# A three-layer network in one launch: the first stage cut into quarters of the features, layer 1's mask on the vector engine, three orders at the tail

## The chip, the cores and the metric

One core of a Trainium2 chip (trn2) runs the whole program in one launch. The metric is the device time of the execution in microseconds (us); lower is better. The kernel before took 763.97 us, the median of 3 runs (763.23 to 764.12). Five engines work side by side, each through its own list of instructions in order: TensorE (PE, with its weight loads PEld), VectorE (DVE), ScalarE (ACT), GpSimd (POOL) and SyncE (SP), which here issues the weight transfers.

## The reference, cut to what matters

The input x is 256 tokens by 1024 features. Each layer normalises x, scales and shifts it by rows made from a conditioning vector c, and projects it. Only the start of layer 0 and the score mask of layer 1 matter here; a third part (mixer and feed-forward) follows.

```python
def rms_norm(x, g):
    return x * rsqrt(mean(x * x, -1) + EPS) * g
...
cond  = silu(c) @ w_ada[layer] + b_ada[layer]     # 3 x 1024: shift, scale, gate
h     = rms_norm(x, norm_g) * (1 + scale) + shift
proj  = h @ w_in          # layer 0: keys and values first (kc, ks, vc, vs | ka, kw, va, vw, gates), then qa ...
...
s = where(mask, q @ k.T * HEAD_DIM ** -0.5, -inf)  # layer 1: one block of 256 keys, causal
p = softmax(s); o = p @ v
x = x + gate * (o * silu(z)) @ w_out
```

## The kernel before

**Numbers.** Every float32 operand of a large product is held as a high part and a low part (`WH`, `WL` for weights, `HH`, `HL` for activations), and one product is three matmuls (`product`, lines 456 to 458). ACT makes the high part with a copy, DVE the low part with a subtraction.

**Pieces.** Weights come in pieces of 128 x 2048 numbers (1 MiB), in the order of `piece_table`. SP issues them in that order; a piece goes either into a ring of three slots (`RAW`) or into a tile that is idle then (`areas`). Before it issues a piece, SP waits until the former user of that place is read (`readers`, `low_done`, `follows`), and everything behind it waits too. `highs(n)` on ACT and `lows(n)` on DVE make the high and low parts of all split pieces up to the n-th (in this order: kcks half 0, kakw half 0, kcks half 1, kakw half 1, then qa half 0 as the fifth and qa half 1 as the sixth).

**First stage (0 to 49 us).** The eight 1 MiB pieces of `ada0_0` to `ada0_3` hold the columns of shift (0, 1) and scale (2, 3), each piece 512 columns by half of the rows of c. `conditioning_half` multiplies a piece by silu(c) in four row groups of TensorE at once; DVE adds the bias (`row_in`), TensorE turns the row into columns (`columns_of`), DVE makes `MOD` and `ADA` (`modulation`). The normalised x (`XH`) is transposed (`norm_turn`), and ACT applies scale and shift while it reads the banks (`first_evict`), then copies the high part into `HH`; DVE makes `HL` (`low_pair`, `low_norm`). Features 0 to 511 come first: pieces 0.0, 0.1, 2.0, 2.1, then `kcks` half 0 against features 0 to 511, and so on for 512 to 1023. `hold_clock` issues transposes that nobody reads.

**After it.** `pair_turn(0)` transposes the rotated kcks heads of token tile 0 and needs DVE's `rotate("kcks", 0)`, which needs ACT's `values_out(0)`. Behind it on TensorE stand `by_tokens("qa", 0)`, `pair_turn(1)` and `key_turns()`. ACT's list there is `values_out(0)`, `highs(5)`, `values_out(1)`, `values_out2(0)`, `highs(6)`; DVE's list is `rotate("kcks", 0)`, `lows(5)`, `rotate("kcks", 1)`, `lows(6)`, `rotate("kakw", 0)`, `rotate("kakw", 1)`.

**Layer 1's attention.** Heads go in eight pairs. `scores(p)` makes 8 matmuls for a pair and then adds the mask with one matmul for each head (line 646); `peaks` on DVE reads the banks; between two pairs TensorE does a projection of some 5 us or more.

**Tail.** `low_stick(3)` on DVE frees what the last of `branch("ato", 0)`'s four blocks on TensorE waits for. Further on, `hidden_tokens(0, 0)` needs the bank that `add_merged(1, 0)` frees, and `hidden_tokens(1, 0)` needs the low part of both halves of `fi1`.

Of the kernel before, what the change touches and what calls it, by code (L numbers as in the profile page):

```python
# [17 lines left out]
ALU = mybir.AluOpType  # L18
# [3 lines left out]
P = 128  # L22
S = 256
NT = S // P
# [20 lines left out]
def piece_table():  # L45
# [19 lines left out]
    t = ada(0, 0, 2) + [first[0][0]] + ada(0, 1) + [first[0][1]] + ada(0, 3) + list(first[1]) + qa[:1]  # L65
    w1v = two("w1v", 8, 256, "raw")
    t += two("w1k", 8, 256, "raw") + qa[1:] + w1v[:1] + qb + w1v[1:] + za[:1]
# [100 lines left out]
def two_blocks_kernel(nc, weights, x_in, consts_in, late_in, cols_in, bada_in, finalg_in, w2_in, sinks_in, gains_in, out):  # L168
# [12 lines left out]
    with ExitStack() as ctx:  # L181
# [110 lines left out]
        placed_in = [sem(f"placed_in{i}") for i in range(19)]  # L292
# [31 lines left out]
        def col(name):  # L324
# [6 lines left out]
        areas = [("ada0_2", 1, [flat(QT[:, :, :])]), ("ada0_1", 1, [flat(V[:, :, :])]), ("ada0_3", 0, [flat(ZS[:, :, :])]),  # L331
                 ("ada0_3", 1, [flat(PROBS[:, :, :])[:, 0:PIECE]]), ("w1k", 0, [flat(PROBS[:, :, :])[:, 0:PIECE]]),
# [118 lines left out]

        @block.tensor
        def _(pe):
# [29 lines left out]
            def half_tokens(name, half, t, width=512, kind="proj", use=None, heads=None, between=None):  # L483
                use = use or f"{name}.{t}"
                bank = tiles[ps.uses[use][0]] if half else ps.open(pe, kind, use)
                in_two = name == "kcks"
                if in_two:
                    pe.wait_ge(first_low, half + 1)
                    if t == 0:
                        pe.wait_ge(pair_low, half + 1)  # L490
                else:
                    wait_parts(pe, name, half)
                for k, w in enumerate(row_blocks(name, half, width)):
                    if between and k == KB // 4:
                        between()
                    if in_two and k == KB // 4:
                        wait_parts(pe, name, half)
                        if t == 0:
                            pe.wait_ge(ht_low, 2 * half + 1)
# [53 lines left out]
            def norm_turn(n, t):  # L553
                for half in range(2):
                    turn(f"n{n}.{t}.{half}", [XH[:, t, (4 * half + j) * P:(4 * half + j + 1) * P] for j in range(4)],
                         [(x_hat, 2 * n + t + 1)], "score" if n == 0 and t else "turn")
# [8 lines left out]
            def conditioning_half(layer, c, half, kind="proj"):  # L565
# [13 lines left out]
                else:  # L579
                    mark_read(mm, name, half)  # L580

# [35 lines left out]
            def pair_turn(t):  # L617
                pe.wait_ge(v_copied, t + 1)
                turn(f"up.{t}", [KR[:, t, 0, :], KR[:, t, 1, :], VCD[:, t, 0, :, :].rearrange("p a d -> p (a d)"),
                                 VCD[:, t, 1, :, :].rearrange("p a d -> p (a d)")], [(roped, t + 1)], ("turn", "out")[t])  # L620
# [9 lines left out]
            def scores(p):  # L630
                pair = (2 * p, 2 * p + 1)
                banks = [ps.open(pe, "score", f"s.{u}") for u in pair]
                for t in range(NT):
                    for u, bank in zip(pair, banks):
# [4 lines left out]
                        pe.matmul(out_, lhsT=half_of(q, QT, q // 2, t * P, (t + 1) * P),  # L639
                                  rhs=half_of(q, KT, kb, 0, (t + 1) * P), start=(t == 0), stop=False)  # L640
# [145 lines left out]
            def hold_clock(n):  # L786

                for _ in range(n):
                    pe.transpose(tiles[1][:, 0:P], ident, ident)

            pe.wait_ge(ident_in, 16)
            hold_clock(6)
            pe.wait_ge(cact_ready, 1)
            conditioning_half(0, 0, 0, "out")
            for t in range(NT):
                norm_turn(0, t)
            conditioning_half(0, 0, 1)
            conditioning_half(0, 2, 0)
            conditioning_half(0, 2, 1)
            hold_clock(5)  # L800
            pe.wait_ge(sel_set, 1)
            first_columns = ps.open(pe, "out", "ada0.0")
            ps.fill(columns_of(first_columns, 0, 0), "ada0.0")
            hold_clock(18)
            half_tokens("kcks", 0, 0, 512, between=lambda: conditioning_half(0, 1, 0, "out"))
            pe.wait_ge(ht_low, 2)
            half_tokens("kcks", 0, 1, 512)
            conditioning_half(0, 1, 1)
            conditioning_half(0, 3, 0)
# [1667 lines left out]
```

## Time and profile before

| what | value |
|---|---|
| median of 3 runs | 763.97 us |
| the profiled execution | 764.18 us |
| its span, first to last instruction | 762.4 us |
| PE busy | 745.4 us (98%) |
| DVE busy | 497.9 us (65%) |
| ACT busy | 380.3 us (50%) |
| transfers | 146.50 MB, mean 192 GB/s |

"Busy" is the time in which the engine had an instruction in flight, so the 98% says where the work is, not that TensorE runs at its peak. The span leaves out 1.8 us around the first and last instruction. Times below are in us from the start of the span. In a timeline a row is: start, length, engine, source line, operation, destination and sources, count, and in brackets how long the engine had been idle and what released it.

### The profile page before, as it was taken

The page shows a single profiled execution, that of the slowest core. Times are in us where ns is not written, and L with a number is a line of the kernel's source. Part 1 is how long each engine was busy: PE and PEld are TensorE (multiplying, and loading weights), DVE is VectorE, ACT ScalarE, POOL GpSimd, SP SyncE. Part 2 cuts the span into 40 slices and gives each one's busy share as a digit, 9 for nine tenths or more (in the row PEclk, how much of TensorE's full clock was granted, in tenths as well). Part 3 has the DMA queues.
Part 4 walks back from the last instruction along what each step waited for, and adds up shares of the span by engine and source line. Part 5 has one row for each costly group of instructions (what it writes and reads, how often), then busy time and mean ns, then how long its engine had stood idle before and what let it go on. Part 6 is the DMA issues. An engine that isn't in the chain of part 4 may idle for free.

```text
span 762.4 us, 12229 instructions
## 1 busy us (share of the span) xinstructions
PE 745.4 (98%) x5039; PEld 641.5 (84%) x5039; DVE 497.9 (65%) x685; ACT 380.3 (50%) x577; POOL 25.6 (3%) x43
## 2 busy tenths in 40 slices
PE   5999999999999999999999999999999999999998
PEld 3687876478888878788999999999878999999886
DVE  1486769638847757884889999647863735546431
ACT  2564476545354756545543444697453544344330
POOL 3000001001000000013000000000000000000000
PEclk9999999999999999999999999999999999999999
DMA  9995348914366373353745554514453654454511
GB/s 367 422 380 184 153 172 326 400 70 144 123 237 242 111 262 126 111 204 117 273 172 185 197 191 166 192 58 138 152 183 135 229 214 183 152 219 173 213 56 55
DMA packets 21959, 146.50 MB, mean 192 GB/s; under 512 B 2589, under 2 KB 2717, under 8 KB 5393
## 3 DMA queue, kind: packets, MB, share of 16 engines
q1 hardware_dynamic: 20880, 142.62, 50.4%
q0 software_dynamic: 752, 2.06, 0.9%
q10 hardware_dynamic: 272, 1.05, 0.3%
q8 instruction: 40, 0.66, 0.3%
q14 instruction: 15, 0.11, 0.0%
HBM read 144.68 MB, written 1.05 MB: 191 GB/s over the span
## 4 chain that ended last, share of the span: by engine, by line
PE 78%; DVE 2%; issue 2%; ACT 0%; POOL 0%; POOLq 0%; DVEq 0%; ACTq 0%
PE banks L456 23%; PE banks L458 22%; PE banks L457 22%; PE banks L550 3%; PE banks L639 1%; PE banks L574 1%; DVE WL L1686 1%; PE banks L678 1%; PE banks L646 1%; PE banks L923 0%; PE banks L908 0%; PE banks L682 0%; DVE KT L1718 0%; PE banks L927 0%; PE banks L925 0%
## 5 line engine op out<-in xcount | busy, mean ns | idle before, releaser
L1686 DVE TENSOR_TENSOR WL<-RAW,WH 128x2048 fp32r<-128x2048 f32 (+1 forms) x103 | 233.6, 2278 | 60.2 <-ACT WH L1170 59.9
L1170 ACT ACTIVATE WH<-RAW 128x2048 fp32r<-128x2048 f32 (+1 forms) x103 | 195.7, 1906 | 72.6 <-PE banks L458 65.6
L456 PE MATMUL banks<-HH,WH 128*128 128x256 f32 x768 | 217.9, 284 | 0.0
L457 PE MATMUL banks<-HL,WH 128*128 128x256 f32 x768 | 217.3, 283 | 0.0
L458 PE MATMUL banks<-HH,WL 128*128 128x256 f32 x768 | 217.3, 283 | 0.0
L457 PEld LDWEIGHTS banks<-HL,WH 128*128 128x128 f32 x768 | 147.3, 192 | 0.1
L456 PEld LDWEIGHTS banks<-HH,WH 128*128 128x128 f32 x768 | 147.3, 192 | 0.1
L458 PEld LDWEIGHTS banks<-HH,WL 128*128 128x128 f32 x768 | 147.3, 192 | 0.0
L456 PE MATMUL banks<-WH,HH 128*128 128x512 f32 (+1 forms) x320 | 127.7, 399 | 1.9 <-DVE WL L1686 0.8
L458 PE MATMUL banks<-WH,HL 128*128 128x512 f32 (+1 forms) x320 | 124.6, 389 | 0.0
L457 PE MATMUL banks<-WL,HH 128*128 128x512 f32 (+1 forms) x320 | 124.5, 389 | 0.0
L456 PEld LDWEIGHTS banks<-WH,HH 128*128 128x128 f32 x320 | 60.4, 189 | 18.4 <-issue 3.3
L458 PEld LDWEIGHTS banks<-WH,HL 128*128 128x128 f32 x320 | 60.3, 189 | 12.6
L457 PEld LDWEIGHTS banks<-WL,HH 128*128 128x128 f32 x320 | 60.5, 189 | 11.1
L2156 DVE SCALAR_TENSOR_TENSOR QT<-HB,COL,QT 128x256 f32<-128x256 f32 x120 | 49.0, 477 | 0.0
L456 PE MATMUL banks<-WH,AH 128*128 128x512 f32 x88 | 34.8, 396 | 0.0
L457 PE MATMUL banks<-WL,AH 128*128 128x512 f32 x88 | 34.8, 396 | 0.0
L458 PE MATMUL banks<-WH,AL 128*128 128x512 f32 x88 | 34.8, 395 | 0.0
L1285 ACT ACTIVATE PROBS<-banks,NM 128x128 f32<-128x128 f32 x40 | 14.5, 364 | 33.1 <-DVE NM L1849 33.1
L1555 ACT ACTIVATE BIG<-banks,GBH 128x256 f32<-128x256 f32 x24 | 10.1, 470 | 34.0 <-PE banks L458 34.0
L1848 DVE TENSOR_REDUCE NM<-banks 128x2 f32<-128x256 f32 x20 | 8.5, 423 | 28.0 <-PE banks L646 28.0
L1141 POOL TENSOR_TENSOR RS<-MS,HALFNEG 128x1 f32<-128x1 f32 (+2 forms) x14 | 12.9, 922 | 409.8 <-DVE MS L1712 145.5
(295 smaller groups left out, 910.6 us busy)
## 6 DMA issues: line engine op xcount, KB each, us to landing
RAW<-in_weights_dram SPq DMA_DIRECT2D x114, 1024.0 KB, 4.8
BIG<-in_weights_dram SPq DMA_DIRECT2D x6, 1024.0 KB, 6.2
ROTS<-in_weights_dram SPq DMA_DIRECT2D x4, 1024.0 KB, 7.2
PROBS<-in_weights_dram SPq DMA_DIRECT2D x2, 1024.0 KB, 11.6
RAW<-in_weights_dram SPq DMA_DIRECT2D x2, 816.0 KB, 10.3
GATE<-in_weights_dram SPq DMA_DIRECT2D x3, 512.0 KB, 9.7
X<-in_x_dram ACTq DMA_DIRECT2D x1, 1024.0 KB, 6.0
QT<-in_weights_dram SPq DMA_DIRECT2D x1, 1024.0 KB, 13.7
```

The lines of the kernel that those rows point to most:

```text
L456: pe.matmul(out_, lhsT=w[0], rhs=x[0], start=start, stop=False, **more)
L457: pe.matmul(out_, lhsT=w[0], rhs=x[1], start=False, stop=False, **more)
L458: return pe.matmul(out_, lhsT=w[1], rhs=x[0], start=False, stop=stop, **more)
L550: mm = pe.transpose(bank[:, j * P:(j + 1) * P], src, ident)
L574: mm = pe.matmul(bank[32 * k:32 * k + 32, :], lhsT=CACT[:, kk, 1 - row:33 - row], rhs=raw_block(name, half, k), start=first, stop=last)
L1141: pool.tensor_tensor(RS[:, n, 0:w], MS[:, n, 0:w], HALFNEG[:, 0:w], ALU.pow).then_inc(rstds, 1)
L1170: do(act.activation(WH[:, home[n], 0:kb * width], RAW[:, slot[n] % RAW_RING, 0:kb * width], ACT.Copy), high_done)
L1285: do(act.activation(PR[:, u % 4, 0:P], bank[:, 0:P], ACT.Exp, scale=-1.0, bias=NM[:, u, 0:1], accum_out=DEN[:, u, 0:1]))
L1555: ins = act.activation(GT[:, f, :], bank[:, b * S:(b + 1) * S], ACT.Tanh, scale=0.5, bias=GBH[:, f:f + 1])
L1686: do(dve.tensor_tensor(WL[:, home[n], w], RAW[:, slot[n] % RAW_RING, w], WH[:, home[n], w], ALU.subtract), low_done)
L1848: do(dve.tensor_reduce(NM[:, pair, 0], both_scores[:, :, 0:P], AX.X, ALU.min))
L2156: ins = dve.scalar_tensor_tensor(CV[:, b, :], src, wk, CV[:, b, :], ALU.mult, ALU.add)
```

## The change

1. The conditioning pieces are cut the other way: `("ada0_c", half, KB, 256, "columns")`, 256 columns by all rows of c. Two pieces (one of shift, one of scale) now give a quarter q of the features (two blocks of 128). The order of the pieces, their places and the releases change with it.
2. The stage's products go quarter by quarter: two blocks for token tile 0, two blocks for tile 1, for kcks and kakw. The transposed half 1 of x is copied from its bank to `QR` (`first_raw`) and scaled from there.
3. On DVE `lows(5)` stands ahead of `rotate("kcks", 0)`; ACT's list is unchanged there. `qa` half 1 is loaded ahead of `w1k`.
4. Layer 1's causal mask is added by DVE in the banks, one instruction for a pair; the two matmuls of a pair go.
5. Tail: `low_stick(3)` ahead of `lows(branch_first + 7)`; `norm_turn(3, 1)` inside `hidden_tokens(1, 0)`; two splits of fi0 and fi1 earlier on ACT and DVE.

```diff
+    quarter = lambda c, half: [(f"ada0_{c}", half, KB, 256, "columns")]
+    t = quarter(0, 0) + quarter(2, 0) + [first[0][0]] + quarter(0, 1) + quarter(2, 1) + [first[0][1]]
+    t += quarter(1, 0) + quarter(3, 0) + [first[1][0]] + quarter(1, 1) + quarter(3, 1) + [first[1][1]] + qa
...
+            def conditioning_quarter(c, half):
+                row, name, use = c // 2, f"ada0_{c}", f"quarter.{2 * (c % 2) + half}"
...
+                for k in range(KB):
+                    g = 32 * (k % 4)
+                    mm = pe.matmul(bank[g:g + 32, 0:256], lhsT=CACT[:, k, 1 - row:33 - row], rhs=raw_block(name, half, k),
+                                   start=row == 0 and k < 4, stop=row == 1 and k >= 4)
...
+            def quarter_columns(q):
+                bank = ps.open(pe, "out", f"ada0.{q}")
+                ps.wait_drained(pe, f"quarter.{q}")
+                for j in (2 * q, 2 * q + 1):
+                    mm = pe.matmul(bank[:, 0:2 * KB].rearrange("p (u b) -> p u b", u=2)[:, :, j],
+                                   lhsT=ACC[:, j * P:(j + 1) * P], rhs=SEL[:, :], start=True, stop=True)
...
+            def quarter_tokens(name, q, t, width, kind):
...
+                pe.wait_ge(*((low_done, first_low)[q % 2 == 0], split[index[(name, half)]] + 1))
+                pe.wait_ge((pair_low, ht_low)[q % 2], 2 * half + t + 1)
+                for k in (2 * q, 2 * q + 1):
+                    mm = product(bank[:, 0:width], [h[:, k, t * P:(t + 1) * P] for h in (HH, HL)],
+                                 row_blocks(name, half, width)[k % 4], k == 0, k == KB - 1)
...
 # TensorE's order
+            conditioning_quarter(0, 0)
+            first_turn(0, 0)
+            first_turn(1, 0)
+            conditioning_quarter(2, 0)
+            first_turn(0, 1)
+            pe.wait_ge(sel_set, 1)
+            quarter_columns(0)
+            first_turn(1, 1)
+            hold_clock(10)
+            kcks(0, 0)
+            conditioning_quarter(0, 1)
+            kcks(0, 1)
+            conditioning_quarter(2, 1)
+            for t in range(NT):
+                ps.wait_drained(pe, f"n0.{t}.1")
+            hold_clock(4, 4)
+            quarter_columns(1)
+            hold_clock(9, 4)
+            kakw(0, 0)
+            kakw(0, 1)
+            conditioning_quarter(1, 0)
+            kcks(1, 0)
+            conditioning_quarter(3, 0)
+            kcks(1, 1)
+            quarter_columns(2)
+            kakw(1, 0)
+            kakw(1, 1)
+            kcks(2, 0)
+            conditioning_quarter(1, 1)
+            conditioning_quarter(3, 1)
+            kcks(2, 1)
+            quarter_columns(3)
+            kakw(2, 0)
+            kakw(2, 1)
+            kcks(3, 0)
+            kcks(3, 1)
+            kakw(3, 0)
+            kakw(3, 1)
             pair_turn(0)
...
 # ACT's order
             first_highs(0, 0)
             first_evict(0, 0)
+            first_evict(0, 1)
             first_highs(0, 1)
+            for t in range(NT):
+                first_raw(t)
+            first_highs(1, 0)
+            first_evict(1, 0)
+            first_evict(1, 1)
+            first_highs(1, 1)
+            first_evict(2, 0)
             first_highs(2, 0)
+            first_evict(2, 1)
             first_highs(2, 1)
+            first_highs(3, 0)
+            first_evict(3, 0)
+            first_evict(3, 1)
+            first_highs(3, 1)
...
 # DVE's order
+            quarter_modulation(0)
             first_lows(0, 0)
+            low_quarter(0, 0)
+            low_quarter(0, 1)
             first_lows(0, 1)
+            quarter_modulation(1)
+            first_lows(1, 0)
+            low_quarter(1, 0)
+            low_quarter(1, 1)
+            first_lows(1, 1)
+            quarter_modulation(2)
+            low_quarter(2, 0)
             first_lows(2, 0)
+            low_quarter(2, 1)
             first_lows(2, 1)
+            quarter_modulation(3)
+            first_lows(3, 0)
+            low_quarter(3, 0)
+            low_quarter(3, 1)
+            first_lows(3, 1)
+            lows(5)
             dve.wait_ge(params_in, 16)
             rotate("kcks", 0)
-            lows(5)
             rotate("kcks", 1)
...
 # layer 1's mask, in peaks on DVE
+                if by_vector(p):
+                    diagonal = both_scores[:, :, 0:TRI].rearrange("p u (b c) -> p u b c", b=3)[:, :, 0:3:2, :]
+                    mask = const("maskw")[:, 0:P].unsqueeze(1).unsqueeze(1).to_broadcast([P, 2, 2, P])
+                    do(dve.tensor_tensor(diagonal, diagonal, mask, ALU.add))
+                    do.after()
...
 # tail, TensorE, then DVE
             hidden_tokens(0, 0)
-            norm_turn(3, 1)
-            hidden_tokens(1, 0)
+            hidden_tokens(1, 0, lambda: norm_turn(3, 1))
...
             conf(3)
+            low_stick(3)
             lows(branch_first + 7)
-            low_stick(3)
...
-            lows(first_split("fi0") + 1)
+            lows(first_split("fi0") + 2)
             low_banks(3, 0)
-            lows(first_split("fi0") + 2)
             add_merged(1, 0)
+            lows(first_split("fi1") + 1)
             add_merged(1, 1)
-            lows(first_split("fi1") + 1)
+            lows(first_split("fi1") + 2)
             stat_merged(1)
             gained_hat("n3", 1, FFNR)
-            lows(first_split("fi1") + 2)
             low_banks(3, 1)
```

## Rows read from the trace of the kernel before

**Rows 1.** What TensorE waited for, 520 to 582 us: longest, times, total.
```profile
PE banks L456 <- DVE AH L2206: 0.9, 1, 0.9
```
**Rows 2.** Busy time by stretch, with counts, granted clock, DMA share, GB/s.
```profile
core 0: us, PE busy (x) PEld busy (x) DVE busy (x) ACT busy (x) POOL busy (x), PEclk, DMA share, GB/s
11.00:13.00 2.00, 2.00 (x13) 1.87 (x10) 0.61 (x7) 0.00 (x0) 0.00 (x0) 1.00 1.04 434
...
21.85:49.08 27.23, 25.89 (x137) 19.22 (x137) 15.55 (x21) 18.16 (x34) 2.14 (x4) 1.00 1.01 416
49.08:56.45 7.37, 7.37 (x44) 6.31 (x42) 6.87 (x16) 2.11 (x8) 0.00 (x0) 1.00 1.00 357
```
**Rows 3.** Timeline of TensorE, 31 to 63 us.
```profile
31.94 1.06 PE L574 MATMUL banks<-PROBS,CACT 128*32 128x512 f32 x8 [0.93 <-DMA PROBS<-in_weights_dram]
...
43.92 0.39 PE L456 MATMUL banks<-WH,HH 128*128 128x512 f32 x1
...
44.60 0.34 PE L456 MATMUL banks<-WH,HH 128*128 128x408 f32 x1
...
49.08 0.38 PE L550 MATMUL banks<-CST,BIG 128*128 128x128 f32 x2
...
55.44 1.26 PE L550 MATMUL banks<-CST,BIG 128*128 128x128 f32 x10
...
62.54 1.07 PE L736 MATMUL banks<-PROBS,ZS 128*32 128x256 f32 x16
```
**Rows 4.** Timeline of TensorE, 9 to 22 us.
```profile
9.27 1.93 PE L574 MATMUL banks<-RAW,CACT 128*32 128x512 f32 x8 [0.74 <-DMA RAW<-in_weights_dram]
11.13 3.68 PE L550 MATMUL banks<-CST,KT 128*128 128x128 f32 x16
...
18.50 1.02 PE L589 MATMUL banks<-SEL,BIG 128*128 128x2 f32 x8 [0.21 <-DVE BIG L1731]
19.38 2.16 PE L789 MATMUL banks<-CST 128*128 128x128 f32 x18
21.85 0.47 PE L456 MATMUL banks<-WH,HH 128*128 128x512 f32 x1 [0.30 <-DVE HL L1973]
```
**Rows 5.** Timeline of DVE and ACT, 17 to 22 us.
```profile
17.66 0.69 DVE L1731 TENSOR_TENSOR BIG<-BIG,banks 128x512 f32<-128x512 f32 x1 [6.05 <-PE banks L574]
...
18.98 1.06 ACT L1222 ACTIVATE WH<-RAW 128x1024 fp32r<-128x1024 f32 x1 [9.87 <-DMA RAW<-in_weights_dram]
...
19.96 0.81 ACT L1201 ACTIVATE ROTS<-banks,ADA,MOD 128x128 f32<-128x128 f32 x2
20.14 1.23 DVE L1963 TENSOR_TENSOR WL<-RAW,WH 128x1024 fp32r<-128x1024 f32 x1 [0.22 <-ACT WH L1222]
20.80 0.42 ACT L1209 ACTIVATE HH<-ROTS 128x256 fp32r<-128x256 f32 x1
...
21.29 0.42 DVE L1973 TENSOR_TENSOR HL<-ROTS,HH 128x256 fp32r<-128x256 f32 x1
```
**Rows 6.** Timeline of ACT, then of DVE, 42 to 46 us.
```profile
42.92 0.36 ACT L1347 ACTIVATE ZS<-banks 128x256 f32<-128x256 f32 x1
...
43.34 1.91 ACT L1170 ACTIVATE WH<-RAW 128x2048 fp32r<-128x2048 f32 x1
...
44.44 0.42 DVE L1791 TENSOR_TENSOR ROTS<-banks,CST 128x256 f32<-128x256 f32 x1
...
45.90 2.28 DVE L1686 TENSOR_TENSOR WL<-RAW,WH 128x2048 fp32r<-128x2048 f32 x1
```
**Rows 7.** Chain of work that ended last, at a pair of layer 1.
```profile
240.00 0.43 PE banks L646 x2
```
**Rows 8.** Timeline at the tail, 533 to 577 us: ACT, DVE, TensorE.
```profile
533.71 0.38 ACT L1543 ACTIVATE AL<-banks 128x256 fp32r<-128x256 f32 x1 [1.64 <-PE banks L941]
...
536.44 0.42 DVE L2206 TENSOR_TENSOR AH<-banks,AL 128x256 fp32r<-128x256 f32 x1
...
569.50 0.47 PE L456 MATMUL banks<-WH,HH 128*128 128x512 f32 x1 [0.43 <-DVE X L2302]
...
576.47 0.47 PE L456 MATMUL banks<-WH,HH 128*128 128x512 f32 x1 [0.36 <-DVE WL L1686]
```

More of the change, by code:

```diff
@@ L291, in two_blocks_kernel @@
         raw_in = [sem(f"raw_in{r}") for r in range(RAW_RING)]
-        placed_in = [sem(f"placed_in{i}") for i in range(19)]
+        placed_in = [sem(f"placed_in{i}") for i in range(20)]
         high_done, low_done, piece_read = sem("high_done"), sem("low_done"), sem("piece_read")
@@ L784, in compressed_turn, with first_turn, hold_clock @@
                               for g in range(2) for t in range(NT)], [(cmp_probs, 1)])
-            def hold_clock(n):
+            def first_turn(t, half):
+                turn(f"n0.{t}.{half}", [XH[:, t, (4 * half + j) * P:(4 * half + j + 1) * P] for j in range(4)],
+                     [(x_hat, t + 1)], "score" if half else "turn")
+            def hold_clock(n, bank=1):
                 for _ in range(n):
-                    pe.transpose(tiles[1][:, 0:P], ident, ident)
+                    pe.transpose(tiles[bank][:, 0:P], ident, ident)
+            kcks = lambda q, t: quarter_tokens("kcks", q, t, 512, "proj")
+            kakw = lambda q, t: quarter_tokens("kakw", q, t, 408, "score")
             pe.wait_ge(ident_in, 16)
@@ L793, in _ @@
             pe.wait_ge(cact_ready, 1)
-            conditioning_half(0, 0, 0, "out")
-            for t in range(NT):
[L796 to L809, printed above, removed]
-            conditioning_half(0, 3, 1)
-            half_tokens("kakw", 0, 0, 408, "turn", between=lambda: conditioning(0, "ada0.1", (1,), "out"))
-            half_tokens("kakw", 0, 1, 408, "out")
-            half_tokens("kcks", 1, 0, 512)
-            pe.wait_ge(ht_low, 4)
-            half_tokens("kcks", 1, 1, 512)
-            half_tokens("kakw", 1, 0, 408)
-            half_tokens("kakw", 1, 1, 408)
+            conditioning_quarter(0, 0)
[11 more added lines that the diff above has]
+            conditioning_quarter(2, 1)
+            for t in range(NT):
+                ps.wait_drained(pe, f"n0.{t}.1")
[22 more added lines that the diff above has]
+            kakw(3, 1)
             pair_turn(0)
@@ L1002, in hidden_tokens @@
                 for k in range(KB):
+                    if between and k == KB // 2:
+                        between()
                     mm = product(out_, [h[:, k, t * P:(t + 1) * P] for h in (HH, HL)],
@@ L1189, in high_norm, with first_raw, first_evict @@
                                       bank[:, :].rearrange("p (b s) -> p b s", b=4), ACT.Copy), ht_high)
-            def first_evict(half, t):
-                act.wait_ge(mod_ready, half + 1)
-                full = (ROT1, ROT2)[t]
+            def first_raw(t):
+                use = f"n0.{t}.1"
+                bank = ps.wait_filled(act, use)
+                ps.drain(act.activation(QR[:, t, :], bank[:, :], ACT.Copy), use)
+            def first_evict(q, t):
+                act.wait_ge(mod_ready, q + 1)
+                full, half = (ROT1, ROT2)[t], q // 2
                 use = f"n0.{t}.{half}"
-                bank = ps.wait_filled(act, use)
                 if half:
-                    act.wait_ge(ht_low, t + 1)
-                for j in range(4):
+                    ps.wait_drained(act, use)
+                    act.wait_ge((pair_low, ht_low)[q % 2], t + 1)
+                    bank = QR[:, t, :]
+                else:
+                    bank = ps.wait_filled(act, use)
+                for j in (2 * (q % 2), 2 * (q % 2) + 1):
                     b = 4 * half + j
```

123 lines of the change are left out of this document (61 added, 62 removed), and 2 rows, old and new, of the table follows.

## The prediction

> **What bounds the kernel now.** I read the waits of TensorE first. It is busy for 98% of the span, and of the waits behind the first stage the one that this change aims at is 0.9 us [rows 1]. So TensorE's list sets the end: each microsecond taken from it is gained, and each microsecond that it waits is lost, wherever it is. The windows then say where it is not full: 27.23 us from the first product at 21.85 to `pair_turn(0)` at 49.08 hold 25.89 us of work, at 416 GB/s, and the next 7.37 us have no hole at all [rows 2]. The first stage is therefore read from the timelines. Until 31.94 it follows the landings (the last conditioning piece releases TensorE there after 0.93 us idle [rows 3]); a piece of 1 MiB takes 1.049 MB / 416 GB/s = 2.5 us [rows 2].
>
> **When the data is there.** The first piece lands at 9.27 [rows 4] and each 1 MiB piece 2.5 us after the one ahead (2.0 us for a kakw piece of 0.84 MB). In the new order that gives, rounded: scale piece of quarter 0 at 11.7, kcks 0 14.2, quarter 1 16.7 and 19.2, kakw 0 21.2, quarter 2 23.7 and 26.2, kcks 1 28.7, quarter 3 31.2 and 33.7, kakw 1 35.7. SP may hold kcks 1 back until DVE has finished kcks 0 (21.2 by the sum below), which is ahead of the 26 us at which the queue would run dry. Below every piece is there at least 2 us before it is used from quarter 1 on: the stage stops being bound by transfers, and the question is what bounds it instead.
>
> **First product.** TensorE starts the first piece at 9.27, 1.86 us until the transposes, and these take 3.68 / 16 = 0.23 each [rows 4]. New: piece to 11.15, eight transposes to 13.0, second piece to 14.9. DVE's row addition is now 256 wide, 0.42 us like the 128x256 row [rows 5]; with hand-offs the columns start at 15.6. Before, the columns start at 18.50 and ACT's scaling at 19.96, 1.46 us later [rows 4, 5]; with half the columns 0.5 less, so 16.55. From there to the first product were 21.85 - 19.96 = 1.9 us (two scalings 0.81, high part 0.42, low part 0.42 and hand-offs) [rows 4, 5]. First product 18.45, against 21.85: 3.4 us earlier.
>
> **The quarters, on TensorE's clock.** Prices: three steps of kcks are 44.60 - 43.92 = 0.68 us, so six matmuls 1.37; 24 of kakw are 49.08 - 44.60 = 4.48 us, so six 1.12; 0.1 more after each wait [rows 3]. A conditioning quarter is eight matmuls of 256 columns in four row groups, as `compress_in` has them: 16 instructions at 62.54, 0.9 us [rows 3]; I take 0.93. Two columns 0.5. DVE's low part of half a kcks piece is 1.23, of half a kakw piece by its size 1.0; ACT's high part 1.06 [rows 5].
> - kcks q0 18.45 to 19.9, piece to 20.85, kcks to 22.2, piece to 23.15. Then nothing is ready: DVE row 0.42, columns at 24.0, scale and shift out by 24.95, and only then, behind them in DVE's list, the low part of kakw 0, to 25.95. kakw q0 at 26.1. Hole: 2.9 less the columns, 2.4 us (the transposes of `hold_clock` lie in it).
> - kakw q0 to 28.45, piece, kcks q1, piece, kcks q1, columns to 33.55, kakw q1 to 35.8. Quarter 2 is scaled from 34.0; on ACT the high part of kcks 1 stands behind it (35.1 to 36.2), and DVE's low part follows to 37.5. kcks q2 at 37.6. Hole: 1.8 us.
> - kcks q2, two pieces, kcks q2, columns to 42.8. Low part of kakw 1 behind the modulation, 43.25 to 44.25. kakw q2 at 44.4. Hole: 1.6 us. kakw q2 to 46.7, kcks q3 of tile 0 to 48.1 (results seen at 48.3), tile 1 49.5, kakw q3 to 51.75.
> The products start 3.4 us earlier and end 51.75 - 49.08 = 2.7 us later. The work between is the same to 1 us; two more of the conditioning pieces now lie behind the first product, and the holes are 5.8 us in place of 1.3 [rows 2].
>
> **The hand-over to qa.** What is late next is `pair_turn(0)`. kcks of tile 0 is complete only 3.45 us before the stage ends. From its results: ACT `values_out(0)` 0.42, then its fifth high part 1.91, then DVE's low part 2.28 (`lows(5)` now stands ahead), then `rotate("kcks", 0)` 45.90 - 44.44 = 1.46 and the last hand-off [rows 6]: 48.3 + 0.45 + 1.95 + 2.3 + 1.65 = 54.75. TensorE has been idle since 51.75: 3.0 us. Behind it `by_tokens("qa", 0)` runs 55.1 to 57.9 and wants `lows(6)`, which ends at 56.2 + 2.3 = 58.5: 0.75 us more. End 61.45, `pair_turn(1)` 0.45, `key_turns` (the last rotation is done at 61.4) at 61.95 against 55.44 [rows 3]. Sum of the first stage: **+6.5 us**. If each hand-off is 0.1 us shorter or longer (some 15 in the chain) that is 5.0 to 8.0. From there on the lists are as before; qb and w1 land before they are used, so the delay stays whole.
>
> **Layer 1's mask.** A pair's two mask matmuls hold the chain for 0.43 us [rows 7]; eight pairs, **-3.4 us**. DVE adds eight additions over 128x512 with a bank as source, 0.69 us each by [rows 5], 5.5 us on an engine that is busy 65% of the time. No row has a write into a bank by DVE. I bound it by the neighbours in size, 0.42 (128x256) below and 1.23 (128x1024) above [rows 5], and take 0.69, the row of its own size and source. The cover is the 5 us of projection that stands between a pair's scores and the turn that needs its probabilities: the peaks come 0.69 - 0.43 = 0.3 us later, well inside. Gain kept between 2.8 and 3.4.
>
> **Tail.** `low_stick(3)`: ACT has its operand at 533.71 + 0.38, DVE does it at 536.44 because a low part of 2.28 stands ahead [rows 8]. Moved, it is done by 534.7, before TensorE asks: the 0.9 us go [rows 1], **-1.0 us** with the restart. What comes later is the low part of a piece that is used some 12 us further on. fi0 and fi1: the 0.43 and 0.36 us idle [rows 8] go or shrink, since `add_merged(1, 0)` no longer stands behind a low part that could have run earlier and the transposes move into the product; against that ACT's square comes some 1.7 us later. I take **-0.7** between 0 and -1.0.
>
> **A rule beside the rows.** After its first work, TensorE's transposes step 0.23 us apart, and 2.16 / 18 = 0.12 apart from 19.38 on [rows 4]; the window 11 to 13 us is nevertheless booked with a granted clock of 1.00, the 2.4 GHz level [rows 2]. The Trainium skill, "TensorE: Matmul & The Clock Gate", Part 1, says that the half rate is the default and that idleness brings it back, 1.2 GHz in place of 2.4. By it the new 3.0 us hole before `pair_turn(0)` could put qa's first products at half rate; the trace of before has no hole of that length behind 21.85, so it shows neither. Worked out as a rival below.
>
> **The sum.** 6.5 - 3.4 - 1.0 - 0.7 = +1.4 us, on the profiled execution's own 764.18 (762.4 of span and 1.8 around it) 765.6; the median is 0.2 below that run, so **765.4 us**. What a measurement of this kernel can tell from no change is 0.2%, 1.5 us; my sum sits at that edge, so this case is split: 54% in all, 24% above the edge and 30% within. Its own range is 763.1 to 767.8 (5.0 or 8.0 for the stage, 2.8 for the masks, 0 or 1.0 for fi).
>
> **Rivals.**
> 1. *Faster: the holes between the quarters do not open.* One mechanism: TensorE's queue of ready work covers the chain of DVE and ACT. For: transfers no longer bind, and DVE and ACT are busy for only 15.55 and 18.16 of 27.23 us [rows 2]. Against: each hole comes from the order of the lists, not from load. With all three closed 5.8 us go: 759.6; it decides once kcks of tile 0 is complete before 45.4 in place of 48.3, which gives 762.5. 22%.
> 2. *Slower: the clock falls in the 3 us hole.* At the half rate TensorE ran from 9.27 to some 14.8, 5.5 us [rows 4]; the same length again costs half of it, 2.8 us: 768.2. 10%.
> 3. *The transfers still bind.* If pieces in the queue share the engines and land together, quarter 0 waits up to one piece, 2.5 us: 767.9. For: DMA is full until 56 us. Against: the first piece is there at 9.27 with three more behind it. 7%, of which 2 within 0.2%.
> 4. *DVE's mask stalls layer 1.* If the addition costs 1.23 us or the peaks are late for ACT, up to 0.3 us a pair comes back: 767.8. 7%, of which 2 within 0.2%.
>
> Faster by over 0.2%: 22%. Within: 30 + 2 + 2 = 34%. Slower: 24 + 10 + 5 + 5 = 44%. The range leaves out the far half of rival 1 and the far ends of the others: 761.0 to 768.3.
>
> **What would show it.** Right: first product near 18.5; holes on TensorE near 24, 36 and 43 us released by a low part (WL); a wait of some 3 us for the rotation before the transposes at 52 to 55; `key_turns` near 62; no row for line 646's form in layer 1; no 0.9 us wait on `low_stick`. Wrong: `key_turns` before 59 or after 64, steps of 0.46 in qa, or waits on DVE in layer 1.

## The result, and the profile after

The changed kernel takes **768.06 us** (median of 6 runs, 767.17 to 770.61), the kernel before beside it on the same chip 763.60 (6 runs, 762.46 to 764.12). The ratio of the runs is **1.0066, interval 1.005 to 1.0081**: some 5.0 us, or 0.7%, slower (4.5 by the two medians). The forecast was 765.4, +1.4 us, inside a range up to 768.3: the sign was right, the size was not. The profiled execution took 768.02 (span 766.2; before 762.4), 3.8 more than that of before.

The waits of TensorE over the whole span of the changed kernel (line; us in total, times, longest):
```profile
...
PE banks L461 <- DVE WL L2045: 3.2, 2, 1.7
PE banks L543 <- DVE BIG L1879: 3.0, 1, 3.0
...
PE banks L461 <- DVE WL L1758: 0.8, 2, 0.4
PE banks L461 <- DVE HL L2055: 0.7, 1, 0.7
```
L2045 is DVE's low part of half a piece of kcks or kakw, L1879 the last operation of `rotate`, L2055 the low part of the scaled tokens. At the tail, 520 to 590 us, the 0.9 us wait of [rows 1] is no longer there; what is left:
```profile
PE banks L461 <- issue: 0.4, 1, 0.4
PE banks L461 <- DVE ZT L2421: 0.2, 1, 0.2
```
The windows that answer to [rows 2], from the first product to the end of the stage and on to `key_turns`, and the twelve matmuls of kakw behind the third hole, most of them at the lower of TensorE's two clock levels (1.2 GHz, where 1.00 is 2.4):
```profile
core 0: us, PE busy (x) PEld busy (x) DVE busy (x) ACT busy (x) POOL busy (x), PEclk, DMA share, GB/s
18.35:54.10 35.75, 32.02 (x217) 24.24 (x217) 13.95 (x24) 18.87 (x40) 2.15 (x4) 0.95 0.90 361
54.10:65.10 11.00, 7.63 (x41) 6.14 (x41) 10.22 (x23) 3.14 (x7) 0.00 (x0) 1.00 0.71 253
45.24:49.10 3.86, 3.86 (x12) 3.80 (x13) 1.86 (x3) 2.83 (x8) 0.00 (x0) 0.56 1.00 395
```
TensorE's timeline, the places of [rows 3] and [rows 4]:
```profile
9.15 1.94 PE L582 MATMUL banks<-RAW,CACT 128*32 128x256 f32 x16 [0.60 <-DMA RAW<-in_weights_dram]
11.02 1.97 PE L543 MATMUL banks<-CST,KT 128*128 128x128 f32 x8
12.92 1.92 PE L582 MATMUL banks<-RAW,CACT 128*32 128x256 f32 x16
14.77 0.66 PE L543 MATMUL banks<-CST,KT 128*128 128x128 f32 x4
...
18.35 0.47 PE L461 MATMUL banks<-WH,HH 128*128 128x512 f32 x1 [0.71 <-DVE HL L2055]
...
19.57 0.39 PE L463 MATMUL banks<-WH,HL 128*128 128x512 f32 x1
19.89 1.07 PE L582 MATMUL banks<-QT,CACT 128*32 128x256 f32 x16
20.89 0.50 PE L461 MATMUL banks<-WH,HH 128*128 128x512 f32 x1
21.23 0.40 PE L462 MATMUL banks<-WL,HH 128*128 128x512 f32 x1
...
26.32 0.42 PE L461 MATMUL banks<-WH,HH 128*128 128x408 f32 x1 [0.50 <-issue]
...
38.31 0.50 PE L461 MATMUL banks<-WH,HH 128*128 128x512 f32 x1 [1.69 <-DVE WL L2045]
...
45.24 0.59 PE L461 MATMUL banks<-WH,HH 128*128 128x408 f32 x1 [1.49 <-DVE WL L2045]
45.62 0.55 PE L462 MATMUL banks<-WL,HH 128*128 128x408 f32 x1
...
57.19 0.41 PE L543 MATMUL banks<-CST,BIG 128*128 128x128 f32 x2 [2.96 <-DVE BIG L1879]
...
60.98 0.50 PE L461 MATMUL banks<-WH,HH 128*128 128x512 f32 x1 [0.41 <-DVE WL L1758]
...
64.27 1.25 PE L543 MATMUL banks<-CST,BIG 128*128 128x128 f32 x10
```
The three holes, stretches in which TensorE has no work that is ready, are where they were foretold (they end at 26.32, 38.31 and 45.24), and so is the hand-over: 2.96 us ahead of `pair_turn(0)`, then 0.41. The last row is `key_turns`: 64.27, against 55.44 in [rows 3].

DVE at the first hole and at the hand-over, and ACT at the hand-over, which answer to [rows 5] and [rows 6]:
```profile
24.82 0.16 DVE L1815 COPY ADA<-banks 128x4 f32<-128x4 f32 x1 [0.76 <-PE banks L595]
25.01 0.16 DVE L1817 SCALAR_TENSOR_TENSOR MOD<-ADA,COL 128x2 f32<-128x2 f32 x1
25.21 1.01 DVE L2045 TENSOR_TENSOR WL<-RAW,WH 128x816 fp32r<-128x816 f32 x1
...
53.07 2.29 DVE L1758 TENSOR_TENSOR WL<-RAW,WH 128x2048 fp32r<-128x2048 f32 x1 [4.53 <-ACT WH L1228]
55.49 0.42 DVE L1870 TENSOR_TENSOR ROTS<-banks,CST 128x256 f32<-128x256 f32 x1
```
```profile
50.68 0.39 ACT L1420 ACTIVATE ZS<-banks 128x256 f32<-128x256 f32 x1 [2.58 <-PE banks L463]
...
51.12 1.92 ACT L1228 ACTIVATE WH<-RAW 128x2048 fp32r<-128x2048 f32 x1
```
The low part at 25.21 stands right behind the modulation at 25.01. At the hand-over ACT waits 2.58 us for the results of kcks with a high part behind them in its list that needs nothing; DVE waits 4.53 for that high part, with the rotation behind it.

The chain at a pair of layer 1, beside [rows 7]:
```profile
246.35 0.86 PE banks L672 x8
247.21 0.59 PE banks L543 x4
247.79 0.23 PE banks L461
```
The mask's 0.43 is gone, but the four transposes that now follow the scores take 0.59. (Where a product follows them, its first step takes 0.43 at 255.23, and 0.24 behind the mask before.) Before, behind the mask, the same chain gave the transposes 0.44:
```profile
240.00 0.43 PE banks L646 x2
240.43 0.44 PE banks L550 x4
```
DVE's mask itself, in its timeline, takes what it was costed at, and TensorE has no wait on it:
```profile
247.35 0.70 DVE L1930 TENSOR_TENSOR banks<-banks,CST 128x512 f32<-128x512 f32 x1 [2.12 <-PE banks L672]
```

**Where the 3.8 us come from.** Difference of the two profiles' clocks at points that answer to each other: `key_turns` +8.83; the first pair of layer 1 (226.92 before) +7.45; the end of its pairs (327.22) +5.25; the turn at 598.83, behind `fi0` and `fi1`, +3.85. So the stage cost 8.8, 1.4 of it came back between 64 and 227 us, the masks gave 2.2, the tail 1.4. What came back is a fall of TensorE's clock that before has in layer 0 and the changed kernel does not: at 157.83, just ahead of it, the difference is still +9.02.
```profile
160.00:165.00 5.00, 5.00 (x27) 3.87 (x27) 0.53 (x2) 1.28 (x3) 0.00 (x0) 0.66 0.00 0
```
That is the kernel before. The changed kernel shows 1.00 from 155 to 180 us and has its fall at 45 us instead. A granted 0.66 over 5 us is 5 x 0.34 = 1.7 us of full clock lost; how much of it reaches the end depends on whether TensorE works or waits in that time.

### The profile page after: what moved, and what is told of

It is laid out like the page before. It is cut to its first block, busy times and chain, and to the rows that moved or that the text cites. A ratio compares the mean times of both kernels' runs of the same rounds, so it can differ in the third digit from the quotient of the medians.

```text
span 766.2 us, 12371 instructions
## 1 busy us (share of the span) xinstructions
PE 744.2 (97%) x5087; PEld 640.6 (84%) x5087; DVE 505.4 (66%) x703; ACT 382.5 (50%) x583; POOL 25.7 (3%) x43
## 3 DMA queue, kind: packets, MB, share of 16 engines
q1 hardware_dynamic: 21024, 142.62, 50.3%
## 4 chain that ended last, share of the span: by engine, by line
PE 79%; DVE 1%; ACT 1%; issue 0%; POOL 0%; ACTq 0%
PE banks L461 23%; PE banks L463 23%; PE banks L462 23%; PE banks L543 3%; PE banks L672 1%; PE banks L567 1%; PE banks L715 1%; DVE WL L1758 1%; PE banks L980 0%; PE banks L965 0%; PE banks L719 0%; PE banks L995 0%; PE banks L683 0%; PE banks L984 0%; PE banks L982 0%; PE banks L970 0%
## 5 line engine op out<-in xcount | busy, mean ns | idle before, releaser
L1758 DVE TENSOR_TENSOR WL<-RAW,WH 128x2048 fp32r<-128x2048 f32 x101 | 229.9, 2288 | 62.8 <-ACT WH L1228 62.4
L1228 ACT ACTIVATE WH<-RAW 128x2048 fp32r<-128x2048 f32 x101 | 192.7, 1914 | 72.9 <-PE banks L463 65.9
L2431 DVE TENSOR_TENSOR AL<-ROTS,AH 128x512 fp32r<-128x512 f32 x9 | 6.2, 692 | 29.0 <-ACT AH L1696 29.0
```

Source lines behind the costliest of these rows:

```text
L1228: do(act.activation(WH[:, home[n], 0:kb * width], RAW[:, slot[n] % RAW_RING, 0:kb * width], ACT.Copy), high_done)
L1758: do(dve.tensor_tensor(WL[:, home[n], w], RAW[:, slot[n] % RAW_RING, w], WH[:, home[n], w], ALU.subtract), low_done)
```

## The experiments

All are compared with the kernel before on their own chip (764.0 to 764.2 there); "ratio" is that of the runs to its runs. A difference from the changed kernel is the difference of the two ratios, where no other source is named; the medians can give up to 1 us more or less, since before's median moves between two groups of times (see the granted clock of each run, below).

**e1: layer 1's masks alone, on the kernel before.** TensorE's mask matmuls are left to layer 0, `peaks` on DVE adds the mask in layer 1.
```diff
+                if by_vector(p):
+                    return
...
+                    do(dve.tensor_tensor(diagonal, diagonal, mask, ALU.add))
```


> The kernel before with one part of the change: layer 1's causal mask added by DVE. Theory (the masks are worth their TensorE time and the changed kernel loses more than I said in its first stage): 3.4 us faster than before. Rival (DVE's addition stalls layer 1 and the mask part is what disappointed): 0 to 1.5 us faster, with waits of TensorE on DVE between 227 and 300 us.

Measured 761.85 (760.43 to 763.17), ratio 0.9973 [0.9962, 0.9984]: -2.1 us, span -2.4. The sign stands, the size does not. Its chain shows the same 0.59 behind the scores:
```profile
238.77 0.86 PE banks L641 x8
239.62 0.59 PE banks L552 x4
...
246.79 0.86 PE banks L641 x8
```
From one pair's scores to the next's are 8.02 us, where before has 8.28 (239.15 to 247.43): 0.26 a pair, 2.1 for eight. I had priced what was removed and not what then stands next to the scores.

**e2: masks and tail on the kernel before**, that is, the changed kernel with the old first stage. ACT's and DVE's lists of `fi0` and `fi1` are as in the change too.
```diff
-            lows(branch_first + 7)
             low_stick(3)
+            lows(branch_first + 7)
...
-            norm_turn(3, 1)
-            hidden_tokens(1, 0)
+            hidden_tokens(1, 0, lambda: norm_turn(3, 1))
```


> The kernel before with layer 1's mask on DVE and the three orders of the tail, so the changed kernel with the old first stage. Theory: 4.9 us faster than before (3.4 and about 1.5), the whole loss is in the first stage, which then costs some 9 us. Rival (the tail gives back what it gains): 3.4 us or less.

Measured 760.78 (759.0 to 761.82), ratio 0.9959 [0.9947, 0.9972]: -3.1 us. The tail is worth 1.0 by the two ratios and 1.4 in the profile of the changed kernel, not 1.7; 4.9 us had been expected of both together. With it the new first stage is isolated: 1.0066 / 0.9959 = 1.0107, **+8.2 us**, where 6.5 was forecast.

**e3: the second and third hole filled.** Twelve unread transposes of a constant ahead of kcks of quarter 2, and twelve ahead of kakw of quarter 2; no list is changed.
```diff
             kakw(1, 1)
+            ps.wait_drained(pe, "n0.0.0"); hold_clock(12, 2)
             kcks(2, 0)
...
             quarter_columns(3)
+            hold_clock(12, 2)
```


> The changed kernel with 12 transposes that nobody reads ahead of kcks of quarter 2 and 12 behind the columns of quarter 3, about 1.4 us each in holes of 1.7 and 1.5 us. Theory (the granted clock fell to 0.56 in kakw of quarter 2 because TensorE stood still before it, and the twelve matmuls took 1.6 us more): 1.6 us less than the changed kernel, granted clock 1.00 from 45 to 49, steps of 0.19 us, and a smaller spread of the runs. Rival (the clock falls for another reason, or varies with the run only): no change in the median, 0.5 in the window.

Measured 766.06 (765.31 to 769.22), ratio 1.0037 [1.0024, 1.0051]: 2.2 us below the changed kernel. The stretch behind the third hole:
```profile
43.98:48.00 4.02, 4.02 (x20) 3.71 (x21) 1.86 (x3) 2.93 (x9) 0.00 (x0) 1.00 1.01 399
```
Granted 1.00 in place of 0.56, steps of 0.19 in place of 0.34. The data comes no earlier and only the idleness is gone, so this agrees with the fall being the hole's doing, at 1.5 to 1.6 us. It does not settle it: e8's profile has the same hole, unfilled, and no fall behind it, and five of e3's eight executions have a mean granted clock below 1.00.

**e4: the hand-over on ACT's side.** ACT's fifth high part goes ahead of the masks' copies and of `values_out(0)`.
```diff
             first_highs(3, 1)
+            highs(5)
             act.wait_ge(params_in, 16)
...
             values_out(0)
-            highs(5)
```


> The changed kernel with ACT's high part of qa half 0 moved ahead of the mask copies and of values_out(0), so that DVE's lows(5) no longer waits for kcks of tile 0. Theory (the hand-over costs 3.0 us idle before the pair turn and 0.75 before the second half of qa): 3.0 to 3.3 us less than the changed kernel, no wait over 0.5 us before the pair turn. Rival (another list takes its place, the rotation itself or the landing of qa): less than 1.5 us.

Measured 764.73 (763.21 to 767.3), ratio 1.001 [1.0, 1.002]: -4.2 us against the changed kernel. By the medians it is 3.3, and 3.0 to 3.3 had been expected. There is no wait ahead of `pair_turn(0)` any more, and holes two and three are untouched (1.70 and 1.50).

**e5: the three low parts.** DVE does the first low part of kakw 0, kcks 1 and kakw 1 ahead of the modulation of quarters 1, 2, 3, ACT the high part of kcks 1 ahead of its scaling; nine unread transposes that lay in the first hole go. The first lines stand for all three quarters.
```diff
-            quarter_modulation(1)
             first_lows(1, 0)
+            quarter_modulation(1)
...
-            first_evict(2, 0)
             first_highs(2, 0)
+            first_evict(2, 0)
```


> The changed kernel with the lists of the first stage turned: DVE's first low part of kakw 0, kcks 1 and kakw 1 ahead of the modulation of quarters 1, 2 and 3, ACT's first high part of kcks 1 ahead of the scaling of quarter 2, and the nine transposes behind the columns of quarter 1 left out. Theory (the holes come from the order of the lists, and the clock falls in them): the three holes shrink from 5.2 us to about 1, the clock stays at 1.00, some 5.5 to 6 us less than the changed kernel, just under before. Rival (the holes come from load or from landings): less than 2 us.

Measured 763.46 (763.09 to 765.99), ratio 1.0001 [0.9989, 1.0013]: -5.0 us against the changed kernel. The waits on L2045 are gone; two short ones, 0.65 and 0.81 us for DVE's row addition ahead of the columns, stand in their place. The clock did not stay at 1.00 as expected: it falls at 50 us (0.66 from 50 to 55) behind the rotation, which still holds TensorE:
```profile
51.33 0.42 PE L543 MATMUL banks<-CST,BIG 128*128 128x128 f32 x2 [3.11 <-DVE BIG L1878]
```

**e6: e4's and e5's edits together.**
```diff
             first_lows(1, 0)
             quarter_modulation(1)
...
             first_highs(3, 1)
+            highs(5)
```


> The same, with ACT's fifth high part also ahead of values_out(0). Theory (holes and hand-over are separate and add up): 3 us less than with the lists alone, so 8.5 to 9 us less than the changed kernel and some 4 less than before. Rival (the hand-over is bound by something that comes with the earlier stage, such as the landing of qa): less than 1.5 us below the lists alone.

Measured 762.59 (761.08 to 763.95), ratio 0.9985 [0.9973, 0.9996]: only 1.2 below e5 where 3 was expected. The two edits do not add. With the holes closed the stage ends at 48.4, in e4 at 52.5, and DVE is next in line: it has low parts of kakw 1 until 45.5 and `lows(5)` until 48.6, so the rotation ends at 50.3, and TensorE still waits 2.08 ahead of 50.44.

**e7: e6 with `kakw(0, 0)` ahead of `quarter_columns(1)`**, four more unread transposes dropped.
```diff
-            hold_clock(4, 4)
-            quarter_columns(1)
             kakw(0, 0)
+            quarter_columns(1)
             kakw(0, 1)
```


> As the last, and on TensorE kakw of quarter 0, tile 0, stands ahead of the columns of quarter 1, in place of the four transposes nobody reads. Theory: another 0.5 to 1 us less, the stage ends near 47 us. Rival (the columns come later and quarter 1 with them): no gain or a loss of up to 1 us.

Measured 761.74 (761.15 to 763.61), ratio 0.9977 [0.9966, 0.9988]: 0.9 below e6 by the medians, but the intervals overlap, and at the same granted clock the two stand level (761.4 and 761.3, see the table of clocks below). The expected 0.5 to 1 us is not shown. TensorE still waits 2.07 us ahead of `pair_turn(0)` at 50.62, this time without a fall of the clock.

**e8: both conditioning pieces of quarter 2 together**, then both tiles of kcks.
```diff
             conditioning_quarter(1, 0)
-            kcks(1, 0)
             conditioning_quarter(3, 0)
+            kcks(1, 0)
             kcks(1, 1)
```


> The changed kernel with both conditioning pieces of quarter 2 next to one another, then kcks of quarter 1 for both tiles. Theory (a change between a conditioning piece and a product costs TensorE about 0.1 us more than I took): the four groups take 0.2 to 0.4 us less than the 5.1 us that they take from 28.7 to 33.8 in the changed kernel; the total moves by no more than that. Rival (a group of six matmuls is slow by itself): the same 5.1 us.

Measured 765.98 (764.68 to 771.57), ratio 1.0035 [1.0016, 1.0054]. In the timeline the four groups take 27.76 to 32.48, 4.72 us, against 28.70 to 33.79, 5.09, in the changed kernel: two changes of kind fewer, 0.37 us less, so 0.18 each. The other 1.7 us of the median are not shown to be this edit's: its profile has no fall behind a third hole of the same 1.49 us, one behind the 2.96 us hole instead, and a shorter start (below).

**e9: the hand-over on DVE's side.** `rotate("kcks", 0)` stands ahead of `lows(5)` again, all else as changed.
```diff
-            lows(5)
             dve.wait_ge(params_in, 16)
             rotate("kcks", 0)
+            lows(5)
```


> The changed kernel with one reordering taken back on VectorE: rotate("kcks", 0) stands ahead of lows(5) again. Theory (the hand-over is a chain, and with the rotation out of it the next link is VectorE's own list): kcks of tile 0 is copied out by ScalarE at 50.68 to 51.1, the rotation takes 1.6 us, so it is done at 52.7, before TensorE ends the stage at 54.1: no wait before pair_turn(0). Then lows(5) 53.07 to 55.35 releases qa at 55.45 (0.9 us wait), and behind the second rotation lows(6) ends at 59.35 and releases its second half (1.2 us wait). key_turns at 62.75 in place of 64.27: 1.5 us of the 3.0 come back, ratio to the changed kernel 0.998, time about 766.5. Rival (the 3.0 us hole is what is lost, and nothing is queued behind it): key_turns near 61.3, -3.0 us, 765.0. Second rival (the reordering was neutral): key_turns stays at 64.3.

Measured 765.87 (765.02 to 766.93), ratio 1.0035 [1.0023, 1.0047]: -2.2 us by the medians. The 2.96 us wait is gone, and two smaller ones on `lows(5)` and `lows(6)` take half of it back:
```profile
55.38 0.47 PE L461 MATMUL banks<-WH,HH 128*128 128x512 f32 x1 [0.84 <-DVE WL L1758]
59.17 0.50 PE L461 MATMUL banks<-WH,HH 128*128 128x512 f32 x1 [0.79 <-DVE WL L1758]
62.48 1.25 PE L543 MATMUL banks<-CST,BIG 128*128 128x128 f32 x10
```
So the theory's chain holds (`key_turns` foretold at 62.75); that the 3.0 us hole were all that is lost does not.

**e10: e6 with its 2.1 us wait filled** by unread transposes.
```diff
             kakw(3, 1)
+            hold_clock(16, 2)
             pair_turn(0)
```


> e6 with sixteen unread transposes of a constant ahead of pair_turn(0), as the kernel has them elsewhere, in the 2.1 us in which TensorE waits for the rotation. Nothing else is changed; the transposes take 16 x 0.12 = 2.0 us, so the wait shrinks to 0.1 us. Theory (the clock falls in this hole in a part of the executions and costs up to 1.4 us there: granted 0.64 in the 4 us behind it in e6's profile): granted clock 1.00 in the 8 us behind it, key_turns near 57.1 in place of 58.4, and a median 0.5 to 1.5 us below e6's, 761.1 to 762.1. Rival (the clock in this place has nothing to do with the hole): the products behind it still step at 0.4 us, and the median stays at 762.6.

Measured 761.47 (761.18 to 763.03), ratio 0.9979 [0.9969, 0.999]. The same four microseconds in e6, then in e10:
```profile
50.40:54.40 4.00, 3.96 (x14) 3.25 (x15) 3.81 (x6) 0.76 (x2) 0.00 (x0) 0.64 1.01 333
```
```profile
50.40:54.40 4.00, 3.51 (x17) 2.70 (x18) 3.76 (x6) 0.76 (x2) 0.00 (x0) 1.00 1.00 324
```
In these two profiles the fall goes with the idleness, but e7 has the same wait and no fall. The median is 1.1 lower, the two ratios' intervals overlap, and executions without a fall take the same 761.3 in both: what differs is how many such executions there are (3 of 12 in e6, 7 of 11 in e10).

**e11: e5 with e9's edit.**
```diff
-            lows(5)
             dve.wait_ge(params_in, 16)
             rotate("kcks", 0)
+            lows(5)
```


> e5 (the changed kernel with the first low parts ahead of the modulations) with rotate("kcks", 0) ahead of lows(5) on VectorE. From e5's profile: the rotation is done at 46.9, the stage ends at 48.2, pair_turn(0) follows at once; lows(5) 47.21 to 49.5 releases qa at 49.6, the second rotation and lows(6) end at 53.5 and release its second half at 53.6: two waits of about 1.3 us in place of one of 3.1. Theory (these two waits are too short for the clock to fall, as the 3.1 us one did in e5): key_turns near 56.9 in place of 59.3, 1.1 us by the chain and 1.3 by the clock: 761.0 to 762.3. Rival (the clock falls after shorter holes too): granted clock below 0.9 in 49 to 58 us, key_turns near 58.2, 762.4.

Measured 762.13 (760.54 to 762.46), ratio 0.9975 [0.9966, 0.9985]: -2.0 against e5. Waits of 0.98 and 0.83 in place of one of 3.11, granted 1.00 from 45 to 60 us, `key_turns` at 56.65 (56.9 foretold).

**e12: e11 with e7's edit.**
```diff
             kakw(0, 0)
+            quarter_columns(1)
             kakw(0, 1)
```


> e11 with the first block of kakw for tile 0 ahead of quarter_columns(1) and its unread transposes dropped, the edit that brought e7 0.8 us below e6. The best form of the new first stage that the study has. Theory: the same 0.8 us again, 760.2 to 761.5; it then stands level with the old first stage with the same masks and tail (e2, 760.8), so that the new order of the first stage is worth nothing by itself once its three holes and the hand-over are mended. Rival (fewer transfers ahead of the first product, 3.4 us earlier, is worth more than the holes that remain): below 759.

Measured 760.81 (760.52 to 763.3), ratio 0.9974 [0.9963, 0.9985]. `key_turns` at 56.86: the edit gave nothing beside e11 (56.65), and at the same granted clock the times are the same too (760.7 and 760.75); the medians differ by 1.3 only since eight of e12's twelve executions have no fall, and five of e11's eleven. It stands beside e2 (0.9959 [0.9947, 0.9972]), whose first stage is the old one; their profiles both span 759.0. **e2 and e12 beat the kernel before by 0.3 to 0.4%, and the new first stage, mended, is worth nothing by the medians.** At the same granted clock it still costs some 1.5 us (762.3 against 760.8 with one fall): e2's `key_turns` is at 55.47, 1.4 ahead of e12's, and the spans are alike only because e2's profile has the fall at 160 us (0.66) and e12's has none.

**The granted clock of each run.** The record has the mean granted clock of every execution. Over a span of 760 us a fall that costs 1.7 us makes it 0.998. The median times, with the number of executions, by that mean:

| kernel | 0.999 to 1.000 | 0.997 to 0.998 | below |
|---|---|---|---|
| before (beside e1 to e12) | 762.6 (27) | 764.2 (44) | 765.3 (11) |
| e1 masks | 760.5 (2) | 761.9 (4) | 763.2 (1) |
| e2 masks and tail | 759.0 (1) | 760.8 (4) | 761.8 (1) |
| changed | none | 768.1 (2) | 768.3 (4) |
| e3 holes filled | 765.5 (3) | 766.2 (3) | 768.4 (2) |
| e8 pieces together | 764.75 (4) | 766.1 (3) | 768.9 (3) |
| e5 low parts first | none | 763.2 (7) | 765.9 (5) |
| e6 = e4 + e5 | 761.3 (3) | 762.1 (4) | 763.8 (5) |
| e10 e6, filled | 761.3 (7) | 763.0 (4) | none |
| e7 | 761.4 (6) | 762.2 (4) | 763.6 (2) |
| e11 = e5 + e9 | 760.7 (5) | 762.25 (6) | none |
| e12 | 760.75 (8) | 762.3 (3) | 763.3 (1) |

So the groups in before's times, near 762.6, 764.2 and 765.3, go with means that fit no fall, one fall and two. In the middle column the changed kernel is 3.9 above before, e1 2.3 below it and e2 3.4.

**The start, in all profiles.** TensorE's first work steps at half the pace (the eight transposes at 11.02 take 1.97 us in the changed kernel, the same eight at 10.69 take 1.09 in e4), although the windows book a granted 1.00 there too, as in [rows 2]. Where that ends differs from one execution to the next. The second conditioning piece in the changed kernel (first row), and in e4:
```profile
12.92 1.92 PE L582 MATMUL banks<-RAW,CACT 128*32 128x256 f32 x16
```
```profile
11.71 1.07 PE L582 MATMUL banks<-RAW,CACT 128*32 128x256 f32 x16
```
The first product is at 18.35 in the one and 16.70 in the other, though the program ahead of it is the same. Over the eleven profiles with the new first stage it lies from 16.62 to 18.35; over the three with the old one only from 21.68 to 21.85: where the slow start ends early there, in e1 and e2, TensorE waits 1.42 us for a landing instead. So `key_turns` is read from the first product. Where the profile has a fall of the clock between, what it cost is taken off. In the third hole that is 1.5 us (in the changed kernel 45.24 to the end of the stage takes 8.84, the same work in e3 7.33). Behind the wait for the rotation it is less, since the fall there lies partly in idle time or takes the place of the wait for `lows(6)`: `pair_turn(0)` to `key_turns` takes 7.08 without a fall, 8.00 in e5, 7.98 in e6 and 7.72 in e8.

| kernel | first product to `key_turns` | without the fall | against changed |
|---|---|---|---|
| changed | 45.9 | 44.4 | |
| e3 holes filled | 44.5 | 44.5 | 0.0 |
| e8 pieces together | 44.7 | 44.1 | -0.4 |
| e9 rotation first | 44.3 | 42.8 | -1.6 |
| e4 high part first | 42.8 | 41.3 | -3.1 |
| e5 low parts first | 42.5 | 41.6 | -2.8 |
| e6 = e4 + e5 | 41.8 | 40.9 | -3.5 |
| e10 e6, filled | 40.6 | 40.6 | -3.8 |
| e11 = e5 + e9 | 39.7 | 39.7 | -4.7 |
| e12 | 40.1 | 40.1 | -4.3 |
| e7 | 39.5 | 39.5 | -4.9 |

Here e4 is worth its 3 us and e5 2.8, both together 3.5 to 3.8 of 5.9, e8 its 0.4, and e3 nothing but the clock. e5 is worth less than the idle time that it closes, since two waits on the row addition remain. e7's figure flatters it: its start is a slow one, its first product at 18.18, and work that hangs on landings did not move with that; its `key_turns` is at 57.71, e10's at 57.56.

## Why the prediction was right in kind and too low in size

- **The transfers stop binding**: right. No wait of TensorE on a landing from 9.15 to the end of the stage.
- **First product 18.45**: 18.35 in this profile; but the step did not see that its time hangs on where the slow start ends (16.62 to 18.35), so that the hit is partly luck of this profile.
- **The holes, 5.8 us in all**: right in place and cause. kakw q0 26.32 (26.1), kcks q2 38.31 (37.6), kakw q2 45.24 (44.4), behind the modulation and the scaling as written. Moving the low parts in e5 closes them, which shows the cause; it gave 2.8 us of the 5.8 that rival 1 put on it. Rival 1 itself ("faster: the holes between the quarters do not open") is out, and so is rival 3, by the first point.
- **"six matmuls 1.37 ... 0.1 more after each wait"**: failed in size. Groups of six between two conditioning pieces take 1.54 and 1.61, a piece 1.00: not only a wait but each change from one kind of matmul to another costs 0.1 to 0.2 us. The prediction's 0.9 for a piece was the distance to the next piece of its own kind (the row in [rows 3] shows a length of 1.07); ahead of a product it is 1.00. Over quarters 0 to 2, 15.2 us (5.15 + 5.09 + 4.94) where I had 14.0: **+1.2**. e8 takes two changes away and gets 0.37 us.
- **The clock**: rival 2 named a fall behind an idle stretch and priced it at 2.8 us in the 3 us hole ahead of `pair_turn(0)`. In this profile it came in the third hole, 1.49 us long, and cost **1.6** (twelve matmuls in 3.88 us; at 0.186 they are 2.24, and in e3 they take 2.34). e3, with the hole filled, has no fall. The Trainium skill, "TensorE: Matmul & The Clock Gate", Part 1, states that idleness brings the half rate back. The trace agrees here (granted 0.56 behind 1.49 us idle), though the same hole in e8 passed without a fall and the fall of before at 160 us has no idle time ahead of it. So what sets a fall off is open.
- **The hand-over**: right. 2.96 idle (3.0), then 0.41 (0.75); `pair_turn(0)` to `key_turns` 7.08 us (7.20). e4 and e9 show the chain from both of its ends.
- **"Sum of the first stage: +6.5 us"** is the failed step: 8.83. The 2.3 us missing are 1.6 of clock and 1.2 of dearer groups, less 0.5 over the first product and the holes. e2 gives 8.2 in the runs. Both lie above the 8.0 at which the prediction ended this term.
- **"-3.4 us" for the masks** is the second: 2.1 in e1 (2.3 at the same granted clock), 2.2 in the profile, below the 2.8 at which the prediction ended it. DVE's price was right (0.69; measured 0.70), the cover held, rival 4 did not come; but the mask matmuls stood between scores and transposes, and without them the transposes cost 0.15 more: 0.43 - 0.15 = 0.28 a pair.
- **Tail, -1.7**: 1.0 to 1.4; the wait on `low_stick(3)` is gone as written.
- Sum: 8.8 - 2.2 - 1.4 = 5.2, less 1.4 for the clock's fall that before has at 160 us and this profile not: 3.8, the difference of the spans. I had not seen that fall in the trace of before, since I read the clock only around the first stage. That the total stayed inside the stated range is luck: without those 1.4 us the profiled execution would have taken 769.4, above 768.3. The fall also makes the groups in before's times, as the granted clock of each run shows; where in the span it lies is known only of the one profile.

## What to carry to other kernels

Finer pieces bring the first product forward, but each one is another round trip from TensorE to DVE and ACT and back: put the work that needs only landed data ahead of every operation in a list that waits for TensorE (e6, the moves of e4 and e5, takes back 5.5 us by the medians, 3.5 to 3.8 of it in the stage itself), and expect such edits not to add, since the next list binds. When small matmuls are taken out from between two kinds, count what the neighbours cost side by side. And read the granted clock over the whole span of the kernel before, and the mean of every run: a fall hides or feigns up to 1.7 us when the change moves it, and two medians can differ only by how many executions had one. Compare executions of the same mean clock.

## What the runs showed that I had not expected

- The clock's fall takes the same 1.7 us of clock wherever it lands (0.66 over 5 us: at 160 in before, e1 and e2; at 45 in the changed kernel and e9; at 50 in e5 and e6), but between 0.6 (e8) and 1.5 us of time up to `key_turns`. A hole of 1.49 us had it in the changed kernel, e4 and e9 but not in e8. Before's stands in a stretch without any idle time, in turns and products of few rows (TensorE busy 5.00 of 5.00 us). e7, with a hole of 2.07 us, had none, nor had e11 and e12, whose waits are about 1 us and less.
- The slow start ends between 10.7 us (in e4, where the transposes at 10.69 already take 1.09 for eight, against 1.97) and some 15 us (in e7, where the four at 14.60 take 0.91, against 0.66); a stage that is no longer bound by transfers passes up to 1.7 us of that on to its end.
- The first step of a product behind another kind of matmul is 0.31 to 0.34 us (0.43 behind the scores) where the rest are 0.23.
